# Retention beside the last twelve projection columns: its side work placed over 20 steps a head instead of 16 or 17

## The chip, the cores and the metric

The kernel runs on one core of a Trainium2 chip. The metric is the device time of one execution in microseconds (us). The engines named here are TensorE (PE: matmuls; PEld: its weight loads), VectorE (DVE), ScalarE (ACT) and SyncE (SP), whose queue issues the loads. Each engine works through its own queue in the program's order, and engines wait for each other only on semaphores.

## What is computed

A sequence of 512 tokens of width 1024 goes through a block with adaptive modulation (a short convolution and a retention mixer side by side, then a feed-forward part), and then through two more layers (a pooling mixer and a gated scan). All is float32. What matters here is the retention mixer, with four heads of 128:

```python
def retention_mixer(q, k, v, g, positions):
    ...
    scores = jnp.einsum('bhncd,bhnmd->bhncm', q, k) * intra_dec[:, None].astype(dt)
    o_intra = jnp.einsum('bhncm,bhnmd->bhncd', scores, v)
    kv = jnp.einsum('bhnmd,bhnme->nbhde', k * k_dec[:, None, :, None].astype(dt), v)
    ...
    _, s_prev = lax.scan(step, jnp.zeros((B, H, dh, dh), jnp.float32), kv)
    o_cross = jnp.einsum('bhncd,nbhde->bhnce', q * q_dec[:, None, :, None].astype(dt), s_prev.astype(dt))
    o = (o_intra + o_cross).transpose(0, 2, 3, 1, 4).reshape(B, S, H, dh)
    of = o.astype(jnp.float32)
    of = of * lax.rsqrt(jnp.mean(of * of, axis=-1, keepdims=True) + EPS)
    ...
    return jax.nn.silu(g) * o
```

## The kernel before

Every large product is made in three passes: each weight tile is split into a high part (ScalarE, L1589) and a low part (VectorE, L918), and PE multiplies high by high, high by low and low by high (L463 to L465). A *column* (`column`, one on each engine) is one 128-wide slice of projection weights. On PE it is 8 steps of three 128x512 matmuls; on VectorE and ScalarE it is the weight work that belongs beside them. On those two engines the weight work stands at step 3 of a column: on VectorE one or two modulation products (L867; these use up weight tiles of `w_ada`), then the low part for the column after next. At step 7 the column's own result is taken from its PSUM bank: `conv_x` on ScalarE, `conv_c` (L1216 to L1221) and `conv_b` (L1227) on VectorE.

The generators are woven by `run(main, side)`: after each step of the column one piece of `side` is issued, up to its next `yield`. So `yield` alone sets at which step a piece stands in its engine's queue. There are twelve columns x, c, b for i = 0 to 3, thus steps 0 to 95, and beside them `side`, which is the retention.

For each head h the pieces are these. PE: the scores (L626, bank 0), the transpose of k (L631, bank 1), the chunk states (L640, bank 1), the inner product (`intra` in the text; L648, bank 2 or 3), the product with the earlier states (`cross`; L655, same bank). VectorE: the scores times the decay mask (L1170), the running sum of the states (L1178, L1181). ScalarE: k scaled (L1820) and four squares with a sum each (L1825).

For each pair of heads, in `retention_norm`: VectorE makes the factors (L1193, the eleven small operations of `root`, L1198); ScalarE scales the two heads' outputs out of banks 2 and 3 (L1838); PE transposes each through bank 7 (L670, `claim(7)` waits until the bank is free); VectorE multiplies it into the gate (L1207), which frees bank 7. Two `gate_row` pieces use bank 7 as well (PE L437; VectorE L896, L898), before columns 3 and 4 on PE, and before columns 4 and 5 on VectorE.

The pair's norm of heads 0 and 1 runs together with head 2 (`both`), that of heads 2 and 3 after head 3. Before the change a head has 16 steps on PE and 17 on VectorE and ScalarE. On PE with base 16h: scores at 0, k at 1, states at 4, intra at 6, cross at 9; norm transposes at steps 41, 44, 73, 76. On VectorE with base 17h: product 0, states 5; factors at 35 and 69, gated products at 45, 48, 79, 82. On ScalarE with base 17h: k at 1, squares at 11; scaling at 36 and 38, 70 and 72.

SyncE loads weight tiles into a ring of five slots; a load is issued when the tile five places ahead in the ring has been used by VectorE.

Of the kernel before, what the change touches and what calls it, by code (L numbers as in the profile page):

```python
# [11 lines left out]
ACT = mybir.ActivationFunctionType  # L12
# [177 lines left out]
def chain(*gens):  # L190
    for g in gens:
        yield from g


def both(a, b):
    for _ in a:
        next(b, None)
        yield
    yield from b
# [8 lines left out]
def build(nc, a):  # L208
    with ExitStack() as ctx:
# [28 lines left out]
        PS = [ctx.enter_context(nc.psum_tensor(f"PS{i}", [128, T], F32)) for i in range(3)]  # L238
# [20 lines left out]
        RO = [Z[:, 20, :], Z[:, 21, :], Z[:, 23, :], TMP[:, 4, :]]  # L259
        GA, G2, GB = COL[:, 16:24], COL[:, 40:48], COL[:, 56:64]  # L260
        RT, R1, RG = COL[:, 48:52], COL[:, 52:56], COL[:, 64:80]
# [86 lines left out]
        banks = Banks([sem(f"s_full{i}") for i in range(8)], [sem(f"s_free{i}") for i in range(8)])  # L348
# [11 lines left out]
        own = Count(sem("s_dve"))  # L360
# [63 lines left out]
        def tensor_program(e):  # L424
# [195 lines left out]
            def retention(h):  # L620


                claim(0)
                e.wait_ge(zdone.sem, zdone.of("qk", 4 + h))
                for c in blocks:
                    m = e.matmul(PS[0][:, c], Z[:, 12 + h, c], Z[:, 8 + h, c], start=True, stop=True)  # L626
                m.then_inc(banks.full[0], banks.fill(("score", h), 0))
                yield
                claim(1)
                for c in blocks[0:3]:  # L630
                    m = e.transpose(PS[1][:, c], Z[:, 12 + h, c], IDN)  # L631
                m.then_inc(banks.full[1], banks.fill(("rkt", h), 1))
                yield
                yield
                yield
                claim(1)
                for j in range(4):
                    e.wait_ge(*banks.taken(("v", j)))
                for i, c in enumerate(blocks[0:3]):
                    m = e.matmul(PS[1][:, c], RKT[:, c], VT[:, i, 128 * h:128 * h + 128], start=True, stop=True)  # L640
                m.then_inc(banks.full[1], banks.fill(("rds", h), 1))
                yield
                yield
                ob = 2 + h % 2
                claim(ob)
                e.wait_ge(*banks.taken(("score", h)))
                for i, c in enumerate(blocks):
                    e.matmul(PS[ob][:, c], RET[:, c], VT[:, i, 128 * h:128 * h + 128], start=i == 0,  # L648
                             stop=i == 0, skip_group_check=True)
                yield  # L650
                yield
                yield
                e.wait_ge(*banks.taken(("rds", h)))
                for i in range(1, 4):
                    m = e.matmul(PS[ob][:, blocks[i]], Z[:, 8 + h, blocks[i]], RST[:, blocks[i - 1]],  # L655
                                 start=False, stop=True, skip_group_check=True)
                m.then_inc(banks.full[ob], banks.fill(("ret", h), ob))
                for _ in range(7):
                    yield

            def retention_norm(h):

                for _ in range(8):
                    yield
                for i in (h, h + 1):
                    yield
                    claim(7)
                    e.wait_ge(*banks.taken(("ret", i)))
                    for c in blocks:
                        m = e.transpose(PS[7][:, c], RO[i][:, c], IDN)  # L670
                    m.then_inc(banks.full[7], banks.fill(("ret norm", i), 7))
                    yield
                    yield

            side = chain(retention(0), retention(1), both(retention(2), retention_norm(0)), retention(3),
                         retention_norm(2))
# [146 lines left out]
            turn, side = iter(()), iter(())  # L823
            for h in range(17):
                steps = project(h) if h < 16 else group(
                    None, [out_bank("hout", t, 0) for t in range(4)], True, "hout")
                for n, _ in enumerate(steps):
# [3 lines left out]
                    if n == 0 and h:  # L831
                        side = mixing(h - 1)
# [14 lines left out]
            for q in range(4):  # L847
                for kk in range(2):
                    m = open_product(first, 2 * q + kk, (3,))
# [5 lines left out]
        def vector_program(e):  # L855
# [308 lines left out]
            def retention(h):  # L1164
                if h:
                    e.wait_ge(*banks.made(("ret", h - 1)))
                else:
                    e.wait_ge(s_d, 16)
                e.wait_ge(*banks.made(("score", h)))
                e.tensor_tensor(RET.rearrange("p (i t) -> p i t", i=4),  # L1170
                                PS[0][:, :].rearrange("p (i t) -> p i t", i=4),
                                DMASK[:, 128 * h:128 * h + 128].rearrange("p (o t) -> p o t", o=1).broadcast_to(
                                    [128, 4, 128]), ALU.mult).then_inc(banks.free[0], 1)
                for _ in range(5):
                    yield

                e.wait_ge(*banks.made(("rds", h)))
                e.tensor_copy(RST[:, 0:128], PS[1][:, 0:128]).then_inc(own.sem, own())  # L1178
                for i in (1, 2):
                    e.wait_ge(own.sem, own.n)  # L1180
                    m = e.scalar_tensor_tensor(out=RST[:, 128 * i:128 * i + 128],  # L1181
                                               in0=RST[:, 128 * i - 128:128 * i], scalar=GAMMA[h] ** 128,
                                               in1=PS[1][:, 128 * i:128 * i + 128], op0=ALU.mult, op1=ALU.add)
                    if i == 1:
                        m.then_inc(own.sem, own())
                m.then_inc(banks.free[1], 1)
                for _ in range(12):
                    yield

            def retention_norm(h):  # L1190
                yield
                e.wait_ge(square.sem, square.of("ret", h + 1))
                e.tensor_scalar(NW[:, 4, 0:8], SSQ[:, 4 * h:4 * h + 8], 1.0 / 128, EPS, ALU.mult, ALU.add).then_inc(  # L1193
                    own.sem, own())
                e.wait_ge(own.sem, own.n)
                root(NW[:, 0, 0:8], 8)
                e.wait_ge(own.sem, own.n)
                e.tensor_tensor(RG[:, 4 * h:4 * h + 8], NW[:, 0, 0:8], GP[:, 4 * h:4 * h + 8], ALU.mult).then_inc(  # L1198
                    own.sem, own("ret", h))
                for _ in range(8):  # L1200
                    yield
                for i in (h, h + 1):
                    yield
                    yield
                    e.wait_ge(*banks.taken(("g", i)))
                    e.wait_ge(*banks.made(("ret norm", i)))
                    e.tensor_tensor(Z[:, 4 + i, :], Z[:, 4 + i, :], PS[7][:, :], ALU.mult).then_inc(  # L1207
                        banks.free[7], 1)
                    yield

            def conv_c(i, b):
                u, y = TMP[:, 1, :], Z[:, i, :]
# [363 lines left out]
        def scalar_program(e):  # L1576
# [237 lines left out]

            def retention(h):
                yield
                if h:
                    e.wait_ge(*banks.made(("rds", h - 1)))
                e.wait_ge(*banks.made(("rkt", h)))
                e.activation(RKT, PS[1][:, 0:384], ACT.Copy, scale=KD[:, h:h + 1]).then_inc(banks.free[1], 1)  # L1820
                for _ in range(10):
                    yield
                e.wait_ge(*banks.made(("ret", h)))
                for c in range(4):
                    m = e.activation(TMP[:, 2 + h % 2, 128 * c:128 * c + 128],  # L1825
                                     PS[2 + h % 2][:, 128 * c:128 * c + 128], ACT.Square,
                                     scale=GP[:, 4 * h:4 * h + 1], accum_out=SSQ[:, 4 * h + c:4 * h + c + 1])
                m.then_inc(square.sem, square("ret", h))
                for _ in range(6):
                    yield  # L1830

            def retention_norm(h):
                yield
                yield
                e.wait_ge(own.sem, own.of("ret", h))
                for i in (h, h + 1):
                    for c in range(4):
                        m = e.activation(RO[i][:, 128 * c:128 * c + 128], PS[2 + i % 2][:, 128 * c:128 * c + 128],  # L1838
                                         ACT.Copy, scale=RG[:, 4 * i + c:4 * i + c + 1])
                    m.then_inc(banks.free[2 + i % 2], 1)  # L1840
                    yield
                    yield

# [8 lines left out]
            def mixed(k):  # L1852

                return banks.taken(("b", k) if k < 4 else ("ret norm", k - 4))

            side = chain(retention(0), retention(1), both(retention(2), retention_norm(0)), retention(3),
                         retention_norm(2))
            for i in range(4):
                run(column(lambda: conv_x(i, 4 + nb % 3)), side)
                run(column(), side)  # L1860
# [346 lines left out]
```

## Time and profile before

| | us |
|---|---|
| median of 3 runs | 1517.99 (1516.59 to 1518.3) |
| profiled execution | 1518.01 |
| its span | 1516.1 |
| PE busy in the span | 1457.7 |
| VectorE busy | 871.7 |
| ScalarE busy | 563.3 |

The page gives busy time by engine, and groups of instructions by line. Busy time of PE is made of overlapping matmuls: one of 128x512 is listed with 0.39 us but the next starts 0.23 us later. The waits view names the engine that waited and whom it waited for. The clock column of the windows is the share of TensorE's full 2.4 GHz that was granted. Times are from the start of the span.

### The profile page before, as it was taken

How to read it: one execution, taken by the hardware profiler on the slowest of the kernel's cores; microseconds unless marked ns; L12 is line 12 of the kernel's file. 1: busy time of each engine (PE TensorE's matmuls, PEld its weight loads, DVE VectorE, ACT ScalarE, POOL GpSimd, SP SyncE). 2: the span in 40 equal slices, each digit the busy share in tenths (PEclk: the TensorE clock that was granted, in tenths of full speed). 3: DMA queues.
4: the chain of work that ended last, by engine and by line, in shares of the span. 5: the costliest groups of instructions: out<-in, count | busy, mean ns of one | idle time of the engine just before them, and what ended most of it. 6: DMA issues, size and time to landing. Idle time of an engine off the chain costs nothing.

```text
span 1516.1 us, 18485 instructions
## 1 busy us (share of the span) xinstructions
PE 1457.7 (96%) x7204; PEld 1211.4 (80%) x7204; DVE 871.7 (57%) x1716; ACT 563.3 (37%) x1022; POOL 0.2 (0%) x4
## 2 busy tenths in 40 slices
PE   5899899899999999999999899999999999999897
PEld 4788777888888888888888787888888888888686
DVE  7786666553333334756457334425778878777435
ACT  6423335422232223543233224333444444445231
POOL 0000000000000000000000000000000000000000
PEclk9999999999999999999999999999999999999999
DMA  8646442263333333124234232332222222222121
GB/s 324 212 152 220 156 139 70 84 228 92 97 98 97 97 98 111 57 97 122 73 97 123 69 95 82 113 95 78 70 68 61 68 70 70 70 70 70 56 70 57
DMA packets 43719, 158.31 MB, mean 104 GB/s; under 512 B 4848, under 2 KB 5232, under 8 KB 43632
## 3 DMA queue, kind: packets, MB, share of 16 engines
q1 hardware_dynamic: 43632, 157.12, 31.9%
q8 instruction: 58, 0.95, 0.3%
q14 instruction: 29, 0.24, 0.1%
HBM read 155.00 MB, written 2.10 MB: 104 GB/s over the span
## 4 chain that ended last, share of the span: by engine, by line
PE 88%; DVE 7%; ACT 3%; issue 1%; DMA 1%; SPq 0%; ACTq 0%; DVEq 0%
PE PS L463 27%; PE PS L465 26%; PE PS L464 26%; PE PS L741 1%; PE PS L789 1%; DVE WL L918 1%; PE PS L752 1%; PE PS L793 1%; PE PS L783 1%; PE PS L761 1%; PE PS L769 1%; DVE RAW L888 1%; PE PS L817 1%; DMA X<-in_x 1%; DVE X L1033 1%
## 5 line engine op out<-in xcount | busy, mean ns | idle before, releaser
L463 PE MATMUL PS<-HH,WH 128*128 128x512 f32 (+1 forms) x1152 | 452.2, 393 | 4.6 <-ACT TMP L1688 2.4
L465 PE MATMUL PS<-HH,WL 128*128 128x512 f32 (+1 forms) x1152 | 437.7, 380 | 0.0
L464 PE MATMUL PS<-HL,WH 128*128 128x512 f32 (+1 forms) x1152 | 436.7, 379 | 0.0
L918 DVE TENSOR_TENSOR WL<-RAW,WH 128x1024 fp32r<-128x1024 f32 x225 | 273.7, 1219 | 82.3 <-ACT WH L1589 82.0
L1589 ACT ACTIVATE WH<-RAW 128x1024 fp32r<-128x1024 f32 x225 | 237.0, 1056 | 174.7 <-PE PS L465 139.3
L463 PEld LDWEIGHTS PS<-HH,WH 128*128 128x128 f32 x1152 | 218.3, 190 | 43.5 <-issue 3.7
L465 PEld LDWEIGHTS PS<-HH,WL 128*128 128x128 f32 x1152 | 217.8, 189 | 41.9
L464 PEld LDWEIGHTS PS<-HL,WH 128*128 128x128 f32 x1152 | 218.5, 190 | 36.9 <-issue 1.0
L463 PE MATMUL PS<-WH,ZH 128*128 128x512 f32 x400 | 156.4, 391 | 3.9 <-issue 3.9
L464 PE MATMUL PS<-WL,ZH 128*128 128x512 f32 x400 | 156.5, 391 | 0.0
L465 PE MATMUL PS<-WH,ZL 128*128 128x512 f32 x400 | 156.4, 391 | 0.0
L965 DVE TENSOR_TENSOR ZL<-Z,ZH 128x512 fp32r<-128x512 f32 x52 | 35.5, 691 | 143.7 <-ACT ZH L1646 143.7
L463 PE MATMUL PS<-WH,HH 128*128 128x512 f32 x224 | 92.6, 413 | 10.9 <-DVE HL L1099 6.2
L463 PEld LDWEIGHTS PS<-WH,ZH 128*128 128x128 f32 x400 | 75.6, 189 | 20.0 <-issue 4.3
L1646 ACT ACTIVATE ZH<-Z 128x512 fp32r<-128x512 f32 x52 | 32.2, 629 | 158.8 <-PE PS L465 158.8
L465 PE MATMUL PS<-WH,HL 128*128 128x512 f32 x224 | 90.1, 402 | 0.0
L464 PE MATMUL PS<-WL,HH 128*128 128x512 f32 x224 | 89.9, 401 | 0.0
L465 PEld LDWEIGHTS PS<-WH,ZL 128*128 128x128 f32 x400 | 75.5, 189 | 15.7
L464 PEld LDWEIGHTS PS<-WL,ZH 128*128 128x128 f32 x400 | 75.4, 189 | 15.8
L1257 DVE TENSOR_TENSOR Z<-TMP 128x512 f32<-128x512 f32 x32 | 22.0, 694 | 90.4 <-ACT TMP L1877 90.3
L463 PEld LDWEIGHTS PS<-WH,HH 128*128 128x128 f32 x224 | 43.8, 196 | 22.4 <-DVE RAW L888 4.2
L1877 ACT ACTIVATE TMP<-PS 128x512 f32<-128x512 f32 x32 | 19.0, 598 | 109.9 <-PE PS L465 109.6
(244 smaller groups left out, 1653.0 us busy)
## 6 DMA issues: line engine op xcount, KB each, us to landing
RAW<-in_w_fc SPq DMA_DIRECT2D x64, 512.0 KB, 3.5
RAW<-in_hgrn_in SPq DMA_DIRECT2D x64, 512.0 KB, 3.5
RAW<-in_ada SPq DMA_DIRECT2D x43, 512.0 KB, 4.6
RAW<-in_pool_in SPq DMA_DIRECT2D x40, 512.0 KB, 3.5
RAW<-in_w_in SPq DMA_DIRECT2D x27, 512.0 KB, 3.8
RAW<-in_pool_out SPq DMA_DIRECT2D x16, 512.0 KB, 3.6
RAW<-in_hgrn_out SPq DMA_DIRECT2D x16, 512.0 KB, 3.5
RAW<-in_w_out SPq DMA_DIRECT2D x8, 512.0 KB, 4.1
```

The source lines that it names most:

```text
L463: e.matmul(out, wh, xh, start=first, stop=False)
L464: e.matmul(out, wh, xl, start=False, stop=False)
L465: return e.matmul(out, wl, xh, start=False, stop=last)
L741: m = e.matmul(PAIR[:, 256 * i:256 * i + 192], t.f[:, c], t.qp[:, i, :], start=True, stop=True)
L752: m = e.matmul(PS[b][:, 64 * i:64 * i + 64].rearrange("p (n l) -> p n l", l=16), t.k[:, c], halves(t.q[:, c], 16)[1], start=True, stop=True)
L761: m = e.matmul(PS[b][0:32, 32 * i:32 * i + 32], k0[:, i, :], q1[:, i, :], start=True, stop=True)
L918: e.tensor_tensor(lo, raw(i), hi.bitcast(F32), ALU.subtract).then_inc(taken.sem, taken(i))
L965: e.tensor_tensor(lo, Z[:, k, :], hi.bitcast(F32), ALU.subtract).then_inc(zlo.sem, zlo(z))
L1257: e.tensor_tensor(Z[:, f, :], TMP[:, f % 2, :], TMP[:, f % 2, :], ALU.mult).then_inc(zdone.sem, zdone("fc1", f))
L1589: e.activation(place(s)[0], raw(i), ACT.Copy).then_inc(whi.sem, whi(s))
L1646: e.activation(z_place(z)[0], Z[:, k, :], ACT.Copy).then_inc(zhi.sem, zhi(z))
L1877: e.activation(TMP[:, f % 2, :], PS[f if f < 4 else f % 7][:, :], ACT.Relu).then_inc(banks.free[f if f < 4 else f % 7], 1)
```

## The change

No instruction is added or taken away. The `yield`s are placed anew so that a head has 20 steps on every engine. The factors move from `retention_norm` into VectorE's `retention` of the pair's second head (a function `retention_factors`), the scaling into ScalarE's `retention` of that head; ScalarE's `retention_norm` is gone. The transposes and the gated products stay in `retention_norm`, beside the next head.

```diff
@@ tensor_program, retention(h), retention_norm(h)
                 m.then_inc(banks.full[1], banks.fill(("rkt", h), 1))
-                yield
-                yield
-                yield
+                for _ in range(4):
+                    yield
                 claim(1)
...
                 yield
                 yield
+                yield
                 ob = 2 + h % 2
...
-                yield
-                yield
-                yield
+                for _ in range(4):
+                    yield
                 e.wait_ge(*banks.taken(("rds", h)))
...
-                for _ in range(7):
-                    yield
-
-            def retention_norm(h):
-
                 for _ in range(8):
                     yield
+
+            def retention_norm(h):
+
                 for i in (h, h + 1):
-                    yield
+                    for _ in range(3):
+                        yield
                     claim(7)
...
-                    yield
-                    yield
+                yield
@@ vector_program, retention(h)
-                for _ in range(5):
+                for _ in range(6):
                     yield
...
                 m.then_inc(banks.free[1], 1)
-                for _ in range(12):
+                for _ in range(9):
                     yield
-
-            def retention_norm(h):
-                yield
+                if h % 2:
+                    retention_factors(h - 1)
+                for _ in range(5):
+                    yield
+
+            def retention_factors(h):
+
                 e.wait_ge(square.sem, square.of("ret", h + 1))
...
-                for _ in range(8):
-                    yield
+
+            def retention_norm(h):
                 for i in (h, h + 1):
-                    yield
-                    yield
+                    for _ in range(4):
+                        yield
...
-                    yield
@@ scalar_program, retention(h)
             def retention(h):
                 yield
+                yield
...
-                for _ in range(10):
+                for _ in range(11):
                     yield
...
-                for _ in range(6):
+                for _ in range(5):
                     yield
-
-            def retention_norm(h):
-                yield
-                yield
-                e.wait_ge(own.sem, own.of("ret", h))
-                for i in (h, h + 1):
-                    for c in range(4):
-                        m = e.activation(RO[i][:, 128 * c:128 * c + 128], PS[2 + i % 2][:, 128 * c:128 * c + 128],
-                                         ACT.Copy, scale=RG[:, 4 * i + c:4 * i + c + 1])
-                    m.then_inc(banks.free[2 + i % 2], 1)
+                if h % 2:
+                    e.wait_ge(own.sem, own.of("ret", h - 1))
+                    for i in (h - 1, h):
+                        for c in range(4):
+                            m = e.activation(RO[i][:, 128 * c:128 * c + 128],
+                                             PS[2 + i % 2][:, 128 * c:128 * c + 128], ACT.Copy,
+                                             scale=RG[:, 4 * i + c:4 * i + c + 1])
+                        m.then_inc(banks.free[2 + i % 2], 1)
+                        yield
+                else:
                     yield
                     yield
...
-            side = chain(retention(0), retention(1), both(retention(2), retention_norm(0)), retention(3),
-                         retention_norm(2))
+            side = chain(*(retention(h) for h in range(4)))
```

## Rows read from the trace of the kernel before

**Rows 1.** The page: busy time of the engines, share of the span, instructions.

```profile
PE 1457.7 (96%) x7204; PEld 1211.4 (80%) x7204; DVE 871.7 (57%) x1716; ACT 563.3 (37%) x1022; POOL 0.2 (0%) x4
```

**Rows 2.** Waits of PE, 105 to 215 us: total, times, longest.

```profile
PE PS L655 <- DVE Z L1181: 2.4, 1, 2.4
PE PS L670 <- ACT Z L1838: 1.6, 1, 1.6
PE PS L648 <- ACT Z L1838: 1.2, 1, 1.2
PE PS L670 <- DVE Z L1207: 1.2, 2, 0.9
```

**Rows 3.** Windows: length, busy us of PE, PEld, DVE, ACT, POOL; clock; DMA.

```profile
152.00:174.00 22.00, 18.08 (x92) 14.74 (x91) 14.34 (x33) 6.28 (x20) 0.00 (x0) 0.92 0.35 120
190.00:202.00 12.00, 9.56 (x46) 7.45 (x45) 10.88 (x25) 3.12 (x9) 0.00 (x0) 1.00 0.43 142
...
121.00:214.00 93.00, 86.64 (x436) 71.59 (x435) 60.64 (x115) 29.60 (x73) 0.00 (x0) 0.98 0.47 165
```

**Rows 4.** Chain that ended last, in order: start, time it added, instruction.

```profile
121.31 0.89 PE PS L626 x8
122.20 0.23 PE PS L463
...
122.90 0.33 PE PS L631 x3
...
125.32 0.67 PE PS L640 x6
...
143.46 0.86 PE PS L437 x2
```

**Rows 5.** Timeline of PE (first row) and VectorE: start, duration, instruction.

```profile
134.97 0.39 PE L463 MATMUL PS<-HH,WH 128*128 128x512 f32 x1
...
135.24 0.69 DVE L1216 TENSOR_TENSOR TMP<-TMP,PS 128x512 f32<-128x512 f32 x1 [4.86 <-PE PS L465]
...
137.94 0.68 DVE L1170 TENSOR_TENSOR Z<-PS,Z 128x512 f32<-128x512 f32 x1
138.54 1.22 DVE L867 SCALAR_TENSOR_TENSOR RAW<-RAW,CB 128x1024 f32<-128x1024 f32 x1
...
163.99 0.28 DVE L1178 COPY Z<-PS 128x128 f32<-128x128 f32 x1
...
164.84 0.68 DVE L896 TENSOR_TENSOR G<-PS,Z 128x512 f32<-128x512 f32 x1
...
166.16 1.22 DVE L867 SCALAR_TENSOR_TENSOR RAW<-RAW,CB 128x1024 f32<-128x1024 f32 x1
...
169.59 0.68 DVE L1207 TENSOR_TENSOR Z<-Z,PS 128x512 f32<-128x512 f32 x1
```

**Rows 6.** Timeline: a square, the first of the factors, the scaling.

```profile
131.05 0.37 ACT L1825 ACTIVATE TMP<-PS,CST 128x128 f32<-128x128 f32 x1 [0.45 <-PE PS L655]
...
156.14 0.16 DVE L1193 TENSOR_SCALAR NW<-SSQ 128x8 f32<-128x8 f32 x1
...
158.15 2.17 ACT L1838 ACTIVATE Z<-PS,COL 128x128 f32<-128x128 f32 x8 [3.49 <-DVE COL L1198]
```

**Rows 7.** Windows as in rows 3, and two PE timeline rows with gaps.

```profile
166.00:168.00 2.00, 2.00 (x9) 1.81 (x8) 2.00 (x4) 1.50 (x8) 0.00 (x0) 0.50 0.00 0
...
262.00:266.00 4.00, 3.73 (x29) 3.31 (x28) 2.84 (x6) 4.00 (x10) 0.00 (x0) 1.00 0.47 135
...
626.00:630.00 4.00, 4.00 (x22) 4.00 (x23) 3.84 (x11) 2.67 (x6) 0.00 (x0) 0.57 0.63 187
...
261.72 0.36 PE L463 MATMUL PS<-HH,WH 128*128 128x256 f32 x1 [2.36 <-ACT TMP L1688]
...
625.85 0.36 PE L463 MATMUL PS<-HH,WH 128*128 128x256 f32 x1 [1.98 <-DVE HL L1050]
```

**Rows 8.** The page's loads: KB each, median us from issue to landing.

```profile
RAW<-in_ada SPq DMA_DIRECT2D x43, 512.0 KB, 4.6
```

More of the change, by code:

```diff
@@ L657, in retention @@
                 m.then_inc(banks.full[ob], banks.fill(("ret", h), ob))
-                for _ in range(7):
+                for _ in range(8):
                     yield
             def retention_norm(h):
-                for _ in range(8):
-                    yield
                 for i in (h, h + 1):
-                    yield
+                    for _ in range(3):
+                        yield
                     claim(7)
@@ L1199, in retention_norm @@
                     own.sem, own("ret", h))
-                for _ in range(8):
-                    yield
+            def retention_norm(h):
                 for i in (h, h + 1):
-                    yield
-                    yield
+                    for _ in range(4):
+                        yield
                     e.wait_ge(*banks.taken(("g", i)))
```

## Prediction

> **What bounds the kernel now.** I read the page first. TensorE (PE) is busy for 96% of the span [rows 1]: time can come only from PE's gaps, or from PE running at a lower clock. Then I read PE's waits over the projection columns beside which the retention runs (121 to 214 us) [rows 2]. There are five: 1.2 + 2.4 + 1.6 + 1.2 = 6.4 us (1.2 is the sum of two, 0.3 and 0.9). The windows agree: over 93 us PE is busy 86.64, and the 6.36 us of idle are those of 152:174 (3.92) and 190:202 (2.44), so that the first two heads have none [rows 3]. The same windows show a clock of 0.92 in 152:174 and 1.00 in 190:202: behind the 2.4 us gap PE fell to 0.50, the 1.2 GHz level [rows 7]. Other engines only matter as releasers: the waits name ScalarE's scaling (L1838), VectorE's state sum (L1181) and the gated product (L1207).
>
> Why they are late is order, not load. One step is three 128x512 matmuls of 0.23 us [rows 4], 0.69; a column is eight. Counting yields gives each side piece its step (0 to 95), and an engine carries out its queue in that order. Before the change, factors of heads 0 and 1 sit at VectorE's step 35, behind the scores' product and the weight work of the column; they begin at 156.14 and the scaling at 158.15 [rows 6], and PE's next intra product (step 38) needs that bank. VectorE's state sum of head 2 is at step 39 behind the convolution, PE's use of it at step 41. The second pair meets the same at steps 69 to 73, and its product at step 79 stands behind the weight work of step 75 while PE wants the bank at step 76.
>
> **The change, part by part.** No instruction is added or removed on any engine, no DMA either; the work and its durations stay. SP's queue is untouched, though the landings it starts follow VectorE's weight work. What moves is steps. After it, for head h with base 20h: PE score +0, transpose of k +1, state +5, intra +8, cross +12; VectorE scores' product +0, state sum +6, for odd h factors +15; ScalarE k scaled +2, squares +13, for odd h scaling +18 and +19. The norm transposes are at PE steps 43, 46, 83, 86, the gated products at VectorE steps 44, 48, 84, 88. The side work ends at step 88 instead of 82, inside the 96.
>
> *The four waits that go.* Let tE be the start of step 40's matmuls on PE, the first of column 5. Side pieces cost PE 0.89 (eight matmuls), 0.67 (six), 0.33 (three transposes), 0.44 for four of them in proportion, and 0.86 a gate row [rows 4]. (1) Intra of head 2 is now at step 48. The factors come at step 35 and wait for squares of head 1 (four of 0.37, some 1.5 us [rows 6], behind PE's cross at step 32): cross 0.67 + squares 1.5 + factors 2.0 (156.14 to 158.15) + eight scalings 2.17 [rows 6] is about 6.4 us, 9 steps; they are done by step 41 or so. Cover is 7 steps, 5 us. (2) Cross of head 2 (step 52) needs the sum at VectorE's step 46: 0.85 us (163.99 to 164.84 [rows 5]) right behind the gated product that ends at tE + 9.0 (below), so tE + 9.9; PE comes at 14.5 (norm 1 at 9.05, then 0.44, two steps, 0.89, four steps): cover 4.6 us. (3) Norm of head 2 (step 83): from PE's start of step 72, convolution product from 0.3 to 0.9, two modulations, a small one and one weight part to 4.5 (3.43 [rows 5] and one of about 0.16 as in [rows 6]), factors to 6.5, four scalings to 7.6. PE gets there at 0.68 + 0.67 + 11 x 0.68 = 8.8: cover 1.2 us, the thinnest. (4) Norm of head 3 (step 86) needs the gated product of head 2 (VectorE step 84), now behind one weight part and not the two modulations too: it ends at 9.9 and PE comes at 11.3. All four priced at zero after; gain 6.4 - 0.3 = 6.1 us.
>
> *The wait that stays and grows.* Bank 7 serves both norms. Norm of head 1 (PE step 46) waits for the gated product of head 0 at VectorE's step 44, and just ahead of that stands step 43 with two modulations and a weight part. VectorE starts at tE + 0.27 (135.24 against PE's 134.97): convolution 2.70 (135.24 to 137.94), gate row 1.32 (164.84 to 166.16), scores' product 0.60 (137.94 to 138.54), weight work 3.43 (166.16 to 169.59), gated product 0.68 [rows 5]: tE + 9.00, and some 0.05 for the hand-over. PE: step 40 0.68, score 0.89, step 41 0.69, k 0.33, two steps 1.38, norm 0.44, two steps 1.38, state 0.67, one step 0.69: tE + 7.16. PE waits **1.9 us**. Before, the same wait shows as 0.3 only, because 1.2 + 2.4 us and a slow clock had been lost ahead of it. What is queued behind it: every matmul of column 5. Norm of head 0 (step 43) needs bank 7 from the gate row at tE + 3.65 and PE arrives at 3.99: no wait, cover 0.3.
>
> *A wait that appears.* PE's second gate row (before step 32) needs bank 7 from VectorE's first one. The state of head 1 is now at step 25, so from its start VectorE gets it after 0.67 and some 0.2, sums for 0.85, works on weights for 3.43 and on the gate row for 0.68: 5.8 [rows 5]. PE takes 0.67 + 2.07 + 0.89 + 2.09 = 5.7. Wait 0.1 to 0.2; I take 0.15. Were a modulation not landed it could be 1.
>
> *The clock.* Price of one fall: a clock of 0.92 over the 22 us of 152:174 is 0.08 x 22 = 1.8 us lost [rows 3]; another fall, 0.57 over the 4 us of 626:630, is 0.43 x 4 = 1.7 [rows 7]. I take 1.7. That fall goes with its gap. Whether the 1.9 us gap brings its own isn't settled by the trace: after a gap of 1.98 the clock was 0.57 over the next 4 us, after one of 2.36 it stayed 1.00 [rows 7], and after 1.6 it stayed 1.00 [rows 2, 3]. From nothing to 1.7; I take nothing, by little. The Trainium skill's "TensorE: Matmul & The Clock Gate", section "HAM oscillation", warns only of idle gaps longer than any of these four; by that rule no fall would come here, which gives the same 1512.0 as my own choice. The trace disagrees with it: the clock fell after 2.4 and 1.98.
>
> *The tail.* Gated product of head 3 is at VectorE step 88, behind the convolution and two low parts; it pushes the last product (step 95) by some 0.25 us. PE wants bank 7 for the output rows only at their eighth product, over 4 us after the last column, and the last of these tiles five row groups later. Zero; if the cover were gone, 0.3.
>
> **Sum.** Profiled execution 1518.01 us (span 1516.1 and 1.9 around it), as the median of three, 1517.99. 1518.01 - 6.38 (all waits) + 1.9 + 0.15 - 1.7 = **1512.0** (1511.98). The stages behind are bound by PE and by their own chains and should move forward unchanged, but where their gaps fall against the clock can differ by one fall of 1.7 either way; the three runs shown spread by as much.
>
> **The rivals.**
> A. As summed: 1512.0, chance 0.42.
> B. The 1.9 us gap brings the clock down: + 1.7, 1513.7. For it: 1.98 did. Against: 2.36 did not. 0.30.
> C. One of the thin covers is gone (1.2 at norm 2, 0.3 at norm 0, a late landing at the gate row): 1.5 to 2 us more atop of B, 1515.5. 0.12.
> D. It doesn't do what it says: spreading moves the waits and PE loses 6 us and a fall again, since VectorE's weight work stands in the same steps (35, 43, 67, 75) as before: 1518. Against it: four of five partners are parted by several steps. 0.07.
> E. The 1.9 is smaller (VectorE starts the convolution's chain sooner, or a fall elsewhere is spared): 1510.3. 0.05.
> F. Slower. VectorE's modulations at step 43 read weights whose slots come free at step 27, and these now come behind the state sum at step 26, 1.5 us later in PE's time. If they landed late, the gated product, norm of head 1 and the whole of column 5 would wait. It decides from 9 us of added wait (8.1 lost before, less 2.05 kept, plus 3). From step 27 to 43 are 16 steps and the pieces between, some 14 us, and a load takes 4.6 [rows 8]; the load would have to take 23. 1521, chance 0.04.
>
> **How the numbers follow.** A measurement of this kernel can tell about 0.2%, 3 us, from no change; the bound for faster is 1515.0. Faster: A + B + E and a quarter of C, 0.80. Within: most of C, D: 0.16. Slower: F, 0.04. Range: from just above E to the upper end of C, 1510.4 to 1515.9, which leaves out D, F, and part of E and C.
>
> **What would show it.** PE's waits in this stretch: L670 for L1207 once, 1.9 us, L437 for L896 0 to 0.3, and neither L648, L655 nor L670 for L1838. If L655 or L648 waits, step (1) or (2) is wrong; if L670 waits for L1838, step (3). The window after the gap tells B from A. VectorE's gated product of head 0 must start right as the weight part ends; if it waits for PE instead, the 1.9 is wrong. PE's busy time there should be as before less 1.7, and the stages behind the output rows unchanged.

## The result, and the profile after

| | us |
|---|---|
| before, median of 4 | 1517.99 (1516.59 to 1518.3) |
| after, median of 4 | 1507.87 (1506.82 to 1509.23) |
| ratio | 0.9936, 95% interval 0.9918 to 0.9953 |
| profiled execution of after, its span | 1509.23, 1507.5 |

The kernel is faster by 10.1 us by the medians (7.1 to 12.4 by the interval), where 6.0 was forecast; 1507.87 lies under the range of 1510.4 to 1515.9. Over all executions on record, 52 of the kernel before and 17 of the changed one, the means are 1516.17 and 1507.63, thus 8.5 us. But the level shifts between the five comparisons (the mean of before lies between 1514.9 and 1517.7), and they do not have the two kernels in equal numbers: inside each comparison the means differ by 9.0 to 9.8 us.

The first question is whether the waits forecast in the retention stretch are the ones in the trace. PE's waits from 105 to 215 us after the change (engine, line, whom it waited for, us in total, times, longest; to be held against [rows 2]):

```profile
PE PS L668 <- DVE Z L1208: 1.7, 1, 1.7
```

The four partners that were to part have parted: no wait for the scaling, none for the state sum, none for the second pair's product. One wait is left, the one forecast at 1.9. The windows say the same with PE's busy time, and the clock column says that no fall came behind that gap (against [rows 3]):

```profile
136.00:152.00 16.00, 15.98 (x78) 12.53 (x77) 11.51 (x26) 4.69 (x12) 0.00 (x0) 1.00 0.53 182
152.00:174.00 22.00, 20.29 (x110) 16.97 (x109) 16.69 (x28) 7.82 (x21) 0.00 (x0) 1.00 0.51 180
...
190.00:202.00 12.00, 12.00 (x59) 9.93 (x58) 7.20 (x16) 6.23 (x14) 0.00 (x0) 1.00 0.49 176
...
121.00:214.00 93.00, 91.27 (x461) 75.87 (x460) 62.77 (x115) 31.05 (x74) 0.00 (x0) 1.00 0.51 179
```

The sum for the wait that stays can be checked instruction by instruction. VectorE's timeline after the change, from the convolution of column 4 to the gated product of head 0, and PE's first transpose behind it (start, duration; as [rows 5]):

```profile
153.73 0.69 DVE L1216 TENSOR_TENSOR TMP<-TMP,PS 128x512 f32<-128x512 f32 x1 [1.35 <-PE PS L465]
...
156.43 0.68 DVE L893 TENSOR_TENSOR G<-PS,Z 128x512 f32<-128x512 f32 x1
157.15 0.69 DVE L895 TENSOR_TENSOR G<-G,Z 128x512 f32<-128x512 f32 x1
157.75 0.68 DVE L1167 TENSOR_TENSOR Z<-PS,Z 128x512 f32<-128x512 f32 x1
158.36 1.22 DVE L864 SCALAR_TENSOR_TENSOR RAW<-RAW,CB 128x1024 f32<-128x1024 f32 x1
...
161.78 0.68 DVE L1208 TENSOR_TENSOR Z<-Z,PS 128x512 f32<-128x512 f32 x1
...
162.51 0.66 PE L668 MATMUL PS<-CST,Z 128*128 128x128 f32 x4 [1.71 <-DVE Z L1208]
```

VectorE runs through without waiting for anybody, as forecast: from 153.73 to 162.46 it takes 8.73 us, the very sum of the prediction. PE arrives at 162.51 - 1.71 = 160.80, 7.3 us after its step 40 began instead of 7.16; hence 1.7 and not 1.9.

So where are the other 4 us? The two profiled executions are 8.8 us apart: 3.5 us in front of the retention, 6.8 us beside it, and 1.7 us lost again behind it, where the clock stayed low for longer after a gap at 844 us. Both programs are the same up to the first retention matmul, the score of head 0. In the profiled execution of before this starts at

```profile
121.15 1.05 PE L626 MATMUL PS<-Z 128*128 128x128 f32 x8
```

and in that of after at

```profile
117.65 1.05 PE L626 MATMUL PS<-Z 128*128 128x128 f32 x8
```

3.5 us lie there, ahead of the change. The gap of PE on which the lead-in hangs, and two windows around it, before:

```profile
46.95 0.77 PE L463 MATMUL PS<-WH,HH 128*128 128x512 f32 x1 [3.82 <-DVE HL L1099]
...
40.00:60.00 20.00, 16.09 (x58) 12.75 (x59) 13.19 (x22) 10.87 (x17) 0.00 (x0) 0.83 0.74 248
```

and after:

```profile
46.12 0.47 PE L463 MATMUL PS<-WH,HH 128*128 128x512 f32 x1 [2.52 <-DVE HL L1096]
...
40.00:60.00 20.00, 17.05 (x74) 13.70 (x74) 14.26 (x22) 12.02 (x18) 0.00 (x0) 1.00 0.80 264
```

Before, the gap was 1.3 us longer and PE ran at 0.83 of its clock over the 20 us; after, at 1.00. The gap ended 0.8 us later before (46.95 against 46.12), and from its end to the first retention matmul it took 74.2 us instead of 71.5: together the 3.5 us. What the gap hangs on is a landing: in the trace of before, VectorE's last modulation product waits for its tile,

```profile
44.96 1.23 DVE L888 SCALAR_TENSOR_TENSOR RAW<-RAW,CB 128x1024 f32<-128x1024 f32 x1 [2.22 <-DMA RAW<-in_ada]
```

and PE waits for what VectorE makes behind it (L1099). The experiments had to say whether this belongs to the change.

### The profile page after: what moved, and what is told of

It is laid out like the page before. It is cut to its first block, busy times and chain, and to the rows that moved or that the text cites. A ratio compares the mean times of both kernels' runs of the same rounds, so it can differ in the third digit from the quotient of the medians.

```text
span 1507.5 us, 18485 instructions
## 1 busy us (share of the span) xinstructions
PE 1454.2 (96%) x7204; PEld 1208.6 (80%) x7204; DVE 871.4 (58%) x1716; ACT 563.1 (37%) x1022; POOL 0.2 (0%) x4
## 4 chain that ended last, share of the span: by engine, by line
PE 89%; DVE 6%; ACT 3%; issue 1%; DMA 1%; SPq 0%; ACTq 0%; DVEq 0%
PE PS L463 27%; PE PS L465 27%; PE PS L464 27%; PE PS L738 1%; PE PS L786 1%; PE PS L749 1%; PE PS L790 1%; PE PS L780 1%; DVE WL L915 1%; PE PS L758 1%; PE PS L766 1%; DVE RAW L885 1%; PE PS L814 1%; DMA X<-in_x 1%; DVE X L1030 1%
## 5 line engine op out<-in xcount | busy, mean ns | idle before, releaser
L463 PE MATMUL PS<-HH,WH 128*128 128x512 f32 (+1 forms) x1152 | 452.1, 392 | 4.4 <-ACT TMP L1688 2.3
L463 PEld LDWEIGHTS PS<-HH,WH 128*128 128x128 f32 x1152 | 218.2, 189 | 43.1 <-issue 3.7
L463 PE MATMUL PS<-WH,ZH 128*128 128x512 f32 x400 | 157.0, 392 | 3.9 <-issue 3.9
L463 PE MATMUL PS<-WH,HH 128*128 128x512 f32 x224 | 91.0, 406 | 9.7 <-DVE HL L1096 5.0
L463 PEld LDWEIGHTS PS<-WH,ZH 128*128 128x128 f32 x400 | 75.7, 189 | 20.1 <-issue 4.3
L463 PEld LDWEIGHTS PS<-WH,HH 128*128 128x128 f32 x224 | 42.8, 191 | 20.7 <-DVE Z L1376 3.7
```

Source lines behind the costliest of these rows:

```text
L463: e.matmul(out, wh, xh, start=first, stop=False)
```

## The experiments

Two lengths are read from each trace and do the work below. The **lead-in** ends with the start of the first retention matmul (L626). The **stretch** goes from there to the first gap behind the output rows, PE's L463 waiting 2.35 us for ScalarE's L1688 ([rows 7] has it at 261.72). It holds all that the change touches.

| trace | lead-in | stretch | PE's waits in the stretch | time |
|---|---|---|---|---|
| before | 121.15 | 140.57 | 6.4, clock fell | 1518.01 |
| x_before | 119.04 | 142.17 | 8.0, clock fell later | 1517.61 |
| x_before2 | 118.38 | 140.60 | 6.4, fell | 1514.67 |
| x_before3 | 117.51 | 140.56 | 6.4, fell | 1514.27 |
| after | 117.65 | 133.73 | 1.7 | 1509.23 |
| x_after | 117.13 | 133.74 | 1.7 | 1506.49 |
| x_after2 | 117.22 | 133.69 | 1.7 | 1505.91 |
| x_after3 | 116.39 | 133.73 | 1.7 | 1507.29 |
| x_after4 | 117.65 | 133.72 | 1.7 | 1506.29 |
| e1_product_first | 121.71 | 131.80 | none | 1511.62 |
| e1_again | 120.38 | 131.77 | none | 1510.12 |
| e1_third | 119.20 | 131.76 | none | 1508.77 |
| e2_spread_only | 119.52 | 137.84 | 3.7, fell | 1512.95 |
| e3_even_16 | 116.99 | 139.87 | 6.1, fell | 1511.89 |
| l_before | 115.54 | 140.57 | 6.4, fell | 1511.76 |
| l_after | 115.14 | 133.71 | 1.7 | 1503.78 |
| p_after | 120.88 | 133.72 | 1.7 | 1510.70 |
| p_e1 | 116.94 | 131.81 | none | 1505.39 |

The stretch repeats within 0.05 us wherever the same waits occur; the lead-in does not repeat. But it comes apart into two pieces that the traces show. One is the end of PE's gap at 46 us: 44.90 to 47.52 us, by the landing. The other is the way from there to the first retention matmul: 71.5 us in the eight traces whose clock stayed at 1.00 from 44 to 54 us (x_before3, the five of the changed kernel, e3_even_16, p_e1), 72.9 to 73.2 in the four with 0.83 there (x_before, x_before2, e1_third, e2_spread_only), 74.1 to 74.2 in the four with 0.66 (before, e1_product_first, e1_again, p_after). The two traces with a lightened lead-in have no such gap. Two executions of the kernel before, x_before2 and then x_before3, with the same gap and another clock behind it:

```profile
45.27 0.47 PE L463 MATMUL PS<-WH,HH 128*128 128x512 f32 x1 [2.08 <-DVE HL L1099]
...
40.00:60.00 20.00, 17.77 (x70) 14.21 (x71) 14.22 (x22) 12.09 (x18) 0.00 (x0) 0.91 0.76 262
...
45.99 0.47 PE L463 MATMUL PS<-WH,HH 128*128 128x512 f32 x1 [2.07 <-DVE HL L1099]
...
40.00:60.00 20.00, 17.93 (x80) 14.52 (x79) 14.31 (x22) 12.08 (x19) 0.00 (x0) 1.00 0.76 265
```

**Both kernels again.** No edit.

> The kernel before, unchanged, for a second trace. Question: the changed kernel gained 10.1 us by the medians, where 6.0 was forecast, and in the two profiled executions 3.5 us of it lie before the first retention matmul (121.15 against 117.65 us from the start), where both programs are the same. Theory L (landing): the lead-in varies from execution to execution, by when the last modulation weights land (one PE gap of 3.8 us in one trace, 2.5 in the other) and where the clock falls. Then this trace puts the first retention matmul somewhere between 117 and 121.5, and the time is 1514 to 1518. Theory S (systematic): the changed program makes its own lead-in shorter. Then this trace has it at 121.1 within 0.3 again, and the time is 1518 within 0.5. Both expect the five waits in the retention stretch again, 6.4 us in sum.

> The changed kernel, unchanged, for a second trace. Theory L: first retention matmul anywhere from 117 to 121.5 us, time 1507 to 1512 on this chip. Theory S: at 117.7 within 0.3, time 1508 within 1. Both expect one wait of 1.7 to 1.9 us (gated product of head 0) in the retention stretch.

x_before: lead-in 119.04, 2.1 us shorter than in the first trace of the same kernel. That is what theory L said and not S (121.1 within 0.3). Its time was 1517.61, within 0.5 of the first all the same, since the stretch was 1.6 us longer. There the gaps of 1.2 and 2.4 us were as before, but the clock fell only behind the third. PE's waits of x_before from 160 to 175 us, and windows around the fall:

```profile
PE PS L655 <- DVE Z L1181: 2.4, 1, 2.4
PE PS L670 <- DVE Z L1207: 1.9, 1, 1.9
...
164.00:166.00 2.00, 2.00 (x12) 1.56 (x9) 2.00 (x4) 1.33 (x8) 0.00 (x0) 1.00 0.00 0
...
168.00:170.00 2.00, 1.80 (x7) 1.61 (x8) 0.15 (x1) 0.00 (x0) 0.00 (x0) 0.63 0.61 205
170.00:172.00 2.00, 2.00 (x6) 1.52 (x6) 0.00 (x0) 0.00 (x0) 0.00 (x0) 0.52 0.97 371
```

With the clock at 1.00 up to 168, PE came 1.6 us sooner to the bank that VectorE had not freed, and waited 1.9 instead of 0.3; then the fall cost its 1.7 as well. In the first trace the fall lay ahead of that wait, and the slow matmuls filled it. So that fall cost almost nothing by itself: without it the waits are 8.0 us and not 6.4. The prediction booked 6.38 us of waits and 1.7 for the fall; together these are the 8.0, so its sum is right here, and only what it puts down to the clock is not. x_after came out at 1507.11 us (ratio 0.9938, 0.9918 to 0.9957), with one wait of 1.7.

**The wait that is left, taken away.**

```diff
             def retention_norm(h):
                 for i in (h, h + 1):
-                    for _ in range(4):
+                    for _ in range(2 if i == 0 else 6 if i == 1 else 4):
                         yield
                     e.wait_ge(*banks.taken(("g", i)))
```

> The changed kernel with VectorE's gated product of head 0 at step 42 instead of 44 (and that of head 1 kept at step 48), so that it stands ahead of the weight work of step 43. Theory of the prediction: the one wait left, 1.7 us, goes and nothing comes in its place: 1.7 us below the changed kernel, or up to 3.4 where the gap also brought the clock down. Rival: bank 7 is held by the weight work only on paper; the next wait in line is the state sum of head 2 (VectorE step 46), which now comes no later than before, or norm 0, and the gap shows there instead: no change within 0.5 us.

PE has no wait in the stretch. The window over it, in e1_product_first:

```profile
121.00:214.00 93.00, 92.97 (x474) 77.66 (x473) 65.52 (x120) 31.96 (x75) 0.00 (x0) 1.00 0.51 176
```

The stretch is 131.80, 1.94 less than with the wait of 1.71. So a gap costs some 0.2 us more than its length. The chain of waits shows where, in the piece right behind a gap. After the change, the transposes behind the 1.7 us gap and eight matmuls without one:

```profile
162.51 0.66 PE PS L668 x4
...
164.55 0.89 PE PS L648 x8
```

Four transposes take 0.66 there and should take 0.44 by the three of 0.33 in [rows 4]; in x_before the same L648 behind a gap is

```profile
157.21 1.16 PE PS L648 x8
```

1.16 against 0.89. The rival (the gap moves on) is out. But the median was 1508.12 (1504.76 to 1511.62), 1 us above x_after's: the traced lead-in was 121.71 against 117.13. A gain of 1.9 us in the stretch did not show in the time, neither here nor over the three comparisons that have both kernels: the means are 1507.71 (13 executions of this variant) and 1507.66 (12 of the changed kernel).

**Half of the change: the spread alone.**

```diff
@@ the head on PE and its first part on VectorE and ScalarE as in the change; then
@@ vector_program, retention(h)
-                for _ in range(12):
+                for _ in range(14):
                     yield
@@ scalar_program, retention(h), behind the squares
-                for _ in range(6):
+                for _ in range(7):
                     yield
```

> Half of the change: every head has 20 steps on all three engines, but factors and scaling stay in the norm that runs beside the next head (factors at VectorE steps 41 and 81, scaling at 42 and 44, 82 and 84, transposes at PE steps 49, 52, 89, 92, gated products at 51, 54, 91, 94). If the spread is what pays (my reading: VectorE's pieces no longer trail PE's), waits are some 2 us (bank 7 behind the weight work of step 51) and the time is within 1 us of the changed kernel. If moving factors and scaling into the pair's own steps is what pays, the scaling is late for the inner product of head 2 again, waits are 4 us or more and the time lies at 1512 to 1516.

Median 1512.39 (1510.08 to 1514.28), ratio 0.997 (0.9957 to 0.9983): slower than x_after by 5.3 us, not within 1. The waits of e2_spread_only:

```profile
PE PS L669 <- DVE Z L1206: 3.5, 2, 2.0
PE PS L648 <- ACT Z L1838: 0.2, 1, 0.2
```

The scaling is late by 0.2 only, so "4 us or more" fails too. Both readings missed. What decides is bank 7 again: the products of heads 0 and 2 stand behind the weight work of steps 51 and 91, PE waits 1.5 and 2.0 us, and behind the second gap the clock falls. Stretch 137.84 = 131.80 + 3.7 + 1.7 for the fall, and 0.6 that is left for the three restarts. The spread takes 2.7 us of the stretch, moving factors and scaling ahead (and with them the norms by 6 steps) another 4.1.

**Even heads without the spread.**

```diff
@@ vector_program, retention(h)
-                for _ in range(12):
+                for _ in range(11):
                     yield
@@ scalar_program, retention(h), behind the squares
-                for _ in range(6):
+                for _ in range(5):
                     yield
```

> The kernel before with one yield fewer in the head's last stretch on VectorE (11 for 12) and on ScalarE (5 for 6), so that a head has 16 steps on all three engines; nothing is spread and nothing moved. It tells apart what evenness alone gives. Theory O (order): state sum of head 2 comes to VectorE's step 37, ahead of the convolution of step 39, and factors to step 33, ahead of the weight work of step 35, so the waits of 1.2 and 2.4 us go; in their place bank 7 is late twice, for norm 0 behind the gate row (1.5 us) and for norm 1 behind the weight work of step 43 (2.3 us). Of the second pair, factors at step 65 stand ahead of step 67 and its 1.6 us goes, the product of head 2 at step 75 stands behind that step's two modulations and its 0.9 grows to 1 to 2. Stretch from the first retention matmul to the first gap behind the output rows: 137 to 139 us, against 140.6 and 142.2 before and 133.7 after. Rival (room): it is the room of 20 steps that pays, evenness gives nothing: five waits, 6 us or more, stretch 140 or more.

Median 1515.36 beside 1514.42 for before: ratio 1.0007 (0.9995 to 1.0018), no change. The waits of e3_even_16:

```profile
PE PS L670 <- DVE Z L1207: 4.6, 2, 2.6
PE PS L670 <- DVE G L896: 1.5, 1, 1.5
```

The waits are at the places theory O named, and the two early ones are gone; their sizes were 1.5, 2.0 and 2.6 against 1.5, 2.3 and 1 to 2. Together 6.1 instead of 6.4, with a fall as before: stretch 139.87, over the 137 to 139 that was expected. One yield each removed 5.2 us of waits (1.2, 2.4 and 1.6) and made 4.9 us anew, all on bank 7. The rival's "6 us or more" was met too, if not its five waits: evenness without the room of 20 steps gave nothing in time.

**More lead-ins.** No edit.

> The kernel before once more, for the lead-in. Theory L: the start of the first retention matmul is drawn anew each time, whatever the kernel: so far 121.15 and 119.04 before, 117.65 and 117.13 after, 121.71 and 119.52 in two variants whose lead-in is the same program. Theory S: before is never under 119, after never over 118. Stretch from there to the gap behind the output rows: 140.6 to 142.2 by both.

> The changed kernel once more, for the lead-in. Theory L: the first retention matmul anywhere between 117 and 122 us. Theory S: 117.1 to 117.7 again. Stretch from there to the gap behind the output rows 133.7 within 0.2 by both, unless the 1.7 us gap brings the clock down this time, then 135.4.

> The kernel before, a fourth trace: as for the third. With it each theory has four lead-ins of before and three of after.

Before had 118.38 and 117.51, so "never under 119" is refuted; the stretches were 140.60, 140.56 and 133.69, as both theories had it. The changed kernel was short again, 117.22.

**The lead-in lightened in both.** Only a quarter of each of the late modulation tiles is loaded; these two kernels leave out the rest, so their output is not the reference's.

```diff
             def load(i):
...
-                e.dma_start(raw(i), a[name][n]).then_inc(s_raw[RSLOT[i]], 16)
+                c = slice(0, 256 if name == "ada" and 11 <= i < 20 else 1024)
+                e.dma_start(raw(i)[:, c], a[name][n][:, c]).then_inc(s_raw[RSLOT[i]], 16)
```

> The kernel before with a lighter lead-in: of eight late modulation tiles (seven or eight of w_ada's, the last that the first modulation reads) only the first quarter of each is loaded, the rest keeps what lay in the slot; so the modulation isn't the reference's. It takes the late landings away, and with them, by theory L, what makes the lead-in vary: the PE gap of 2 to 3.8 us at about 46 us shrinks to under 1.5, the first retention matmul lies at 114 to 117 us, and the times spread by less (3 us or so, not 7). If the spread stays, landings aren't its source.

> The changed kernel with the same lighter lead-in. By theory L the difference of the two light kernels is that of the retention stretch alone: 6.9 us (or 8.4 where the clock fell late in the stretch), thus 6.5 to 8. By theory S, that the changed program shortens its own lead-in by some 2 us beyond this, 9 to 10 remain.

The gap at 46 us is gone. The window in l_before, to be held against the 16.09 busy and 0.83 above:

```profile
40.00:60.00 20.00, 19.44 (x83) 15.35 (x83) 15.64 (x26) 13.13 (x19) 0.00 (x0) 1.00 0.80 256
```

The lead-ins are 115.54 and 115.14. The times of l_before spread by 2.3 us over ten executions (1511.76 to 1514.08), where those of the kernel before on the same chip spread by 5.7 over thirteen (1513.35 to 1519.09). So late landings, and the clock that falls behind their gap, are the larger part of the spread of the kernel before. For the changed kernel this is not shown: four executions of l_after still spread by 3.1 us (1503.40 to 1506.53), and four of x_after3 on the same chip by 3.2. With the late landings away the medians are 1512.33 and 1504.69: 7.6 us, inside 6.5 to 8 and not the 9 to 10 of theory S. The stretches differ by 6.86.

**Draws, or a level of each program?** x_after3, e1_again, x_after4 and e1_third have no new edit; p_after and p_e1 add one small instruction behind the last work.

```diff
                 e.scalar_tensor_tensor(out=flat(2 * t), in0=X[:, t, :], scalar=RT[:, t:t + 1], in1=G[:, :],
                                        op0=ALU.mult, op1=ALU.mult).then_inc(zdone.sem, zdone("final", t))
+            e.memset(GB, 0.0)
```

> The changed kernel a fourth time, for its lead-in and its spread. Nine times so far lie between 1505.9 and 1509.2 us, while those of before spread from 1512.6 to 1520.3. Theory L: the first retention matmul somewhere from 117 to 122 us, and with more executions some of the times reach 1510 to 1512. Theory S: 117.1 to 117.7 again, no time over 1509.5.

> The variant with the gated product of head 0 ahead of the weight work, beside the changed kernel on one chip. In its trace the retention stretch was 131.8 us against 133.7, yet its median was 1 us higher, as its lead-in was 121.7 against 117.1. Theory L: with more executions it comes out 1 to 2 us below the changed kernel, and its lowest time 1 to 2 us below that one's lowest. Theory S: its lead-in is long by itself, and it stays level or above.

> The changed kernel again. If lead-ins are draws of one distribution (theory L): first retention matmul anywhere from 116 to 122, and over these four kernels no ranking. If each program has its own level (theory S): 116.4 to 117.7 a fifth time, times 1505.7 to 1509.3.

> The variant with the gated product first, again. Theory L: anywhere from 116 to 122 us. Theory S: 120 to 122 a third time, and a median not below the changed kernel's although its retention stretch is 1.9 us shorter.

> The changed kernel with one memset of a 128x8 tile behind VectorE's last work (0.2 us at most, beside the last output). Theory L: as the changed kernel. Theory S in its plain form (level by the program's image): a level of its own, which may be 119 to 122; if it is short again like the changed kernel's and the next is long like e1's, the level would go with the order of the retention work, which comes later than the lead-in, and neither theory explains it.

> The variant e1 with the same memset. Theory L: anywhere; with a short lead-in the time is 1504 to 1506, the lowest of all. Theory S: its own level, not that of e1.

Medians: x_after3 1506.93 and e1_again 1507.24 beside 1516.15 for before; x_after4 1508.99, e1_third 1507.35, p_after 1508.64 and p_e1 1507.07 beside 1517.89. With the memset the changed kernel had a long lead-in, 120.88, and e1 a short one, 116.94. So the order of the retention work is not what shortens or lengthens the lead-in. That each binary has a level of its own is not refuted: the changed kernel was short in five traces of five (116.4 to 117.7) and its 17 times end at 1509.66, e1 long in three of three (119.2 to 121.7), while one and the same binary of before covered 117.5 to 121.2. In e1's three traces the clock fell behind the gap at 46 us each time, in the five of the changed kernel never. As forecasts of the time both theories missed: L had e1 1 to 2 us below the changed kernel, and its median was 0.3 above in one comparison (x_after3, e1_again) and 1.6 below in the next (x_after4, e1_third), where S had it not below. What makes the clock fall there in one execution and not in another stays open.

## Why the prediction was right and wrong

**What bounds the kernel, and the four waits that go: right.** All four are gone in every trace of the changed kernel. Three of the four covers were near the forecast. The first was much larger: head 2's inner product began 10.0 us after the scaling had ended (164.55 against 152.41 + 2.18), where 5 us were forecast, as its seven steps were counted at 0.69 us each, without the side pieces and the wait between them. The thinnest, norm of head 2, was priced at 1.2 us. ScalarE's scaling of the first pair, then of head 2, and PE's transposes after the change:

```profile
152.41 2.18 ACT L1836 ACTIVATE Z<-PS,COL 128x128 f32<-128x128 f32 x8 [1.10 <-DVE COL L1199]
...
191.10 1.14 ACT L1836 ACTIVATE Z<-PS,COL 128x128 f32<-128x128 f32 x4 [2.50 <-DVE COL L1199]
...
193.49 0.60 PE L668 MATMUL PS<-CST,Z 128*128 128x128 f32 x4
```

191.10 + 1.14 against 193.49 is 1.2 us.

**The wait that stays: right,** 1.7 for 1.9, at the place and with the cause named; e1 shows it by taking it away. **The wait that appears** was 0.15 in the sum and is not there (PE busy 15.98 of 16 in 136:152). **The clock behind the gap:** it stayed at 1.00 in all seven traces with that gap (the five of the changed kernel, l_after, p_after), so A and not B. The Trainium skill's "TensorE: Matmul & The Clock Gate", section "HAM oscillation", warns only of idle gaps longer than this one. These seven traces agree with it; e2_spread_only does not, as the clock fell there behind a gap of 2.0 us.

**The size of the stretch: too small by 0.9.** The sum gave 6.0 and the traces give 6.86. Waits: 6.4 - 1.7 = 4.7 (4.3 forecast, as 1.9 and 0.15 were left to wait). The fall: 1.7 as forecast. The rest, 0.5, is a term that the sum left out: what a gap costs beside its length. There are four gaps fewer, thus some 0.1 us each, where e1's single gap gave 0.2 and e2's three 0.6 together; that the term is there is shown, its size a gap is not.

**The step that failed** is the base of the sum: "Profiled execution 1518.01 us (span 1516.1 and 1.9 around it), as the median of three, 1517.99." Every term was taken off this one number, so what lies ahead of the stretch was carried over as it stood, without a reason; the spread of the three runs was read as one fall of the clock in the stages behind. The lead-in was 121.15 us in that execution, and 117.5 to 119.0 in the three later traces of the same kernel; 52 times of it run from 1512.62 to 1520.27. The trace held the warning, which the prediction does not mention: 3.8 us of waiting for a landing, followed by a clock of half. Against a base of 1516.17 (the mean of 52) the sum would have given 1510.1, and with the true stretch 1509.3, against a measured mean of 1507.63.

What the runs showed in its place adds up. The four traces of the kernel before and the five of the changed one have mean times of 1516.14 and 1507.04 us, 9.1 apart, as inside the comparisons. Of these, 7.25 lie in the stretch (6.9, and 8.4 in the one trace where the clock fell late), 1.8 in the lead-in (119.0 against 117.2), and nothing behind (1254.3 in both, though single traces differ by up to 3 us there). Of the 1.8, 0.4 is the end of the landing gap, and 1.4 is the clock, which fell behind that gap in three of the four traces of before and in none of the five after. With the lead-in lightened 7.6 are left between the medians. Whether the changed binary is favoured in the lead-in by more than luck isn't settled; p_after, with the same retention, had the fall and a lead-in of 120.88.

**The rivals.** B, C, D and F did not occur. E named "a fall elsewhere is spared" with 0.05 and 1510.3; that one might be spared ahead of the stretch, and that more than one length there varies, is what was missed. The chances of faster (0.80) hold; the range was too narrow, as no case in it moved the base.

## What to carry to other kernels

When pieces of side work are woven into an engine's queue by step, list each engine's order and put every release next to what stands ahead of it: one yield decided over 5 us of waits, and a gain in one place (e3) comes back as a wait on the next shared buffer. Compare a trace with a trace over the stretch that the change touches, which repeated within 0.05 us here while whole times moved by 7. A single profiled execution is a sample of its lead-in: look at what in it hangs on landings, and where the clock fell, before taking it as the base.

## What the runs showed of the hardware

A PE gap cost 1.94 us for 1.71 of waiting; eight 128x128 matmuls took 1.16 us behind a gap and 0.89 without one.

A fall of the clock ahead of a wait is nearly free, as slow matmuls fill what would have been waited (stretch 140.6), and costs nearly all of its 1.7 us when it comes behind (142.2). The stages behind the output rows say the same in all 18 traces: from the end of PE's gap of 2.35 us there to the end of its next wait it is 13.58 to 13.60 us, whether the clock stayed at 1.00 (four traces, the next wait 3.9 us) or fell (fourteen, the next wait 2.4 to 3.3).

The length of a single gap did not decide whether the clock fell behind it. It stayed at 1.00 behind 1.71 us (seven traces), 2.02 (e3_even_16), 2.35 (four of the 18 traces, behind the output rows), 2.41 (x_before) and 3.08 (x_after4, at 46 us). It fell behind 1.98 ([rows 7]), 2.01 (e2_spread_only), 2.35 (the other fourteen), 2.41 (before) and 2.61 (e3_even_16).

Loads of the same 512 KB tiles in the same order landed at different times from one execution to the next: PE's gap for the last modulation was 1.35 us and ended at 44.90 in x_after3, and was 3.61 and ended at 47.52 in e1_product_first. Loading a quarter of each took the gap away.
